# First projection fed from the unscaled, pre-transposed input in three pieces; value product of the attention moved behind the projection

## What is computed

```python
h = rmsnorm(x, norm1_g)
proj = h @ w_in + b_in                    # 1024 -> 4352 columns
qa, ka, va, qb, kb, vb, ga, gb = split(proj)
oa = neighborhood_attention(qa, ka, va, na_rpb)   # 8 heads of 64
ob = sliding_window_gqa(rope(qb), rope(kb), vb, swa_sinks)
merged = sigmoid(ga) * (oa @ w_up_a) + sigmoid(gb) * (ob @ w_up_b)
x = x + merged @ w_out
h2 = rmsnorm(x, norm2_g)
x = x + moe_clamped_swiglu(h2, ...)       # top 4 of 32 experts, 1024 -> 2048 -> 1024
return rmsnorm(x, final_g)
```

## Time and profile before

| | |
|---|---|
| runs | 1160.08, 1163.53, 1163.86 us |
| the profiled execution | 1160.33 us |
| its span on the core | 1158.4 us |
| TensorE busy in the span | 94% |
| VectorE, ScalarE, GpSimd busy | 22%, 12%, 1% |
| bytes moved | 436.4 MB |

### The profile page before, as it was taken

How to read it: one execution, slowest core, us unless ns; L and a number is a source line. 1 busy time by engine, 2 the same in 40 slices (tenths; PEclk the granted TensorE clock), 3 DMA queues, 4 the chain that set the end, 5 groups by cost and what they waited for, 6 DMA issues and landing times.

```text
span 1158.4 us, 13079 instructions
## 1 busy us (share of the span) xinstructions
PE 1087.3 (94%) x5169; PEld 475.6 (41%) x5169; DVE 250.2 (22%) x531; ACT 139.9 (12%) x267; POOL 16.3 (1%) x21
## 2 busy tenths in 40 slices
PE   7999999999999999999999999999999999999997
PEld 6887778633333333333333333233333333333332
DVE  2253532231111111111111111111111111211112
ACT  0121420210100000000000000000001111111111
POOL 0200000200000000000000000000000000000000
PEclk9999999999999999999999999999999999999999
DMA  8963373499999999999999999999999999999993
GB/s 280 354 257 109 100 291 145 186 398 390 430 427 429 429 427 429 429 427 429 429 427 429 429 427 429 429 427 429 429 427 429 428 426 427 430 428 428 427 430 136
DMA packets 42565, 436.41 MB, mean 377 GB/s; under 512 B 11650, under 2 KB 12084, under 8 KB 13396
## 3 DMA queue, kind: packets, MB, share of 16 engines
q1 hardware_dynamic: 42548, 436.16, 90.4%
HBM read 435.10 MB, written 1.05 MB: 377 GB/s over the span
## 4 chain that ended last, share of the span: by engine, by line
PE 60%; DMA 35%; DVE 2%; ACT 1%; issue 1%; POOL 0%; SPq 0%; DVEq 0%; POOLq 0%; ACTq 0%
DMA ring<-in_w 35%; PE bank L733 24%; PE bank L764 10%; PE bank L492 9%; PE bank L654 3%; PE bank L702 3%; PE bank L577 2%; PE bank L613 2%; PE bank L660 2%; PE bank L488 1%; DVE work L1090 1%; PE bank L539 1%; ACT held L1139 1%; PE bank L525 1%; PE bank L720 1%
## 5 line engine op out<-in xcount | busy, mean ns | idle before, releaser
L733 PE MATMUL bank<-ring,work 128*64 128x512 f32 x2048 | 452.5, 594 | 28.3 <-DMA ring<-in_w 27.6
L733 PEld LDWEIGHTS bank<-ring,work 128*64 128x64 f32 x2048 | 143.7, 137 | 316.4 <-issue 253.6
L764 PE MATMUL bank<-ring,work 128*64 128x512 f32 x1024 | 233.8, 598 | 18.1 <-DVE work L1090 18.1
L764 PEld LDWEIGHTS bank<-ring,work 128*64 128x64 f32 x1024 | 67.8, 136 | 140.7 <-issue 115.0
L1082 DVE TENSOR_SCALAR work<-bank 128x512 f32<-128x512 f32 x32 | 22.1, 691 | 435.0 <-PE bank L733 435.0
L492 PE MATMUL bank<-hT,ring 128*128 128x256 f32 x464 | 103.0, 381 | 0.8 <-DVE hT L833 0.8
L492 PEld LDWEIGHTS bank<-hT,ring 128*128 128x128 f32 x464 | 87.3, 190 | 16.1 <-issue 1.9
L1204 ACT ACTIVATE work<-work 128x512 f32<-128x512 f32 x32 | 20.1, 630 | 559.2 <-DVE work L1082 559.2
L1093 DVE COPY work<-bank 128x512 f32<-128x512 f32 x32 | 22.1, 692 | 253.7 <-PE bank L764 253.7
L654 PE MATMUL bank<-hT,work 128*64 128x512 f32 x264 | 64.6, 610 | 0.0
L702 PE MATMUL bank<-work 64*128 64x512 f32 x256 | 63.6, 615 | 0.9 <-DVE work L1093 0.9
(11 more groups left out here) (176 smaller groups left out, 451.2 us busy)
## 6 DMA issues: line engine op xcount, KB each, us to landing
ring<-in_w SPq DMA_DIRECT2D x182, 2048.0 KB, 21.6
ring<-in_w_in SPq DMA_DIRECT2D x17, 1024.0 KB, 12.9
held<-in_w SPq DMA_DIRECT2D x10, 1024.0 KB, 11.1
ring<-in_w SPq DMA_DIRECT2D x10, 1024.0 KB, 16.8
ring<-in_w_out SPq DMA_DIRECT2D x4, 1024.0 KB, 5.1
ring<-in_w_up_a SPq DMA_DIRECT2D x2, 1024.0 KB, 11.2
ring<-in_w_up_b SPq DMA_DIRECT2D x2, 1024.0 KB, 7.2
tables<-in_na_rpb SPq DMA_DIRECT2D x16, 96.0 KB, 4.9
```

The lines of the kernel that those rows point to most:

```text
L733: last = pe.matmul(bank[CAP * a:CAP * (a + 1), bk, :], kT, pairs[:, pair_of(k // 2), at + q * 512:at + (q + 1) * 512], start=False, stop=k ...
L764: last = pe.matmul(bank[CAP * a:CAP * (a + 1), BH, :], fT, pairs[:, pair_of(c), at + a * 512:at + (a + 1) * 512], start=f == 0, stop=f == ...
```

## The change

1. The host hands over `x` also transposed (`xT`, laid where `x` goes later), the columns `vec`, and the bias table at full size in plain order, with the mask in plain order too; so `from_right` and the transposes at the start go.
2. `xT` and chunk 0 of `w_in` are loaded in three alternating pieces: two blocks of 128 rows, two, and four (`FIRST`). VectorE multiplies a block by `norm1_g` into `xg1`, and `project_first` multiplies piece by piece. Chunks 0 and 1 use this unscaled input, chunk 2 and later use `hT`, which is `xg1` times the scale of each token.
3. The scale: ScalarE squares `xT`, VectorE sums over the blocks, TensorE sums over the partitions (`sum_squares`) inside chunk 1, GpSimd takes the power, VectorE makes two diagonal matrices, TensorE spreads them over the partitions (`spread_scale`), also inside chunk 1. VectorE multiplies what it reads of chunks 0 and 1 by it.
4. ScalarE's queue issues `vec`, `ident`, `v_bias` and `sink_b`. One DMA of 1.5 MiB takes the place of the sixteen of 96 KB. Row-ordered `x` (1 MiB) is loaded behind chunk 12, for the residual sum.
5. In the loop over c the order is `turn_probs`, `scores`, `project(c)`, `attend`. The first unit's scores stand at c = 5, the rotary step at c = 10, units 4 to 7 at c = 12 to 15, their transpositions at c = 13 to 16. VectorE reads an output one chunk later. PSUM banks are assigned anew (`BK`, `BF`, `BQ`, `BR`, `UPB`, `OUTB`).
6. The first lifting product no longer waits for the last gates and the last four outputs; the second and third take over these waits.

The diff, cut to its core:

```diff
+        xT = x.rearrange("p m d -> p (m d)").rearrange("p (k t) -> p k t", t=T)
+        xg1 = gates[:, 0:KD, :]
+        square = hT
...
-        ROPE_C = GATE_C
-        UNIT_C = [4, 6, 7, 8, 11, 12, 13, 14]
-        TURN_C = [6, 7, 8, 9, 12, 13, 14, 15]
+        ROPE_C = GATE_C + 1
+        UNIT_C = [5, 6, 7, 8, 12, 13, 14, 15]
+        TURN_C = [6, 7, 8, 9, 13, 14, 15, 16]
         unit_at = lambda table, c: table.index(c) if c in table else None
         LAST_PLAIN = TURN_C[-1]
-        BS, BT, BO, BK = 3, 5, 7, 2
+        BS, BT, BO, BK = 3, 5, 7, 3
+        BF, BQ, BR = 4, 6, 7
+        UPB = [4, 2, 0, 6]
+        OUTB = [2, 3, 0, 1]
+        FIRST = [slice(0, 2), slice(2, 4), slice(4, KD)]
...
+        def projected(c, a):
+            return half_(BF)[:, 1, :] if (c, a) == (0, 1) else half_(c % 3)[:, a, :]
...
-            for m in range(MT):
-                sp.dma_start(x[:, m, :], x_in[0, m * P:(m + 1) * P, :]).then_inc(x_landed[m], 16)
-            sp.dma_start(C("ident"), consts[:, CONST["ident"]]).then_inc(ident_landed, 16)
-            sp.dma_start(vec_rows[0:D_IN // P, :], b_in.rearrange("l (b p) -> (l b) p", p=P)).then_inc(vec_landed, 16)
-            for i, g in enumerate((norm1_g, norm2_g)):
-                at = D_IN // P + i * KD
-                sp.dma_start(vec_rows[at:at + KD, :], g.rearrange("l (b p) -> (l b) p", p=P)).then_inc(vec_landed, 16)
+            for n, ks in enumerate(FIRST):
+                cols = slice(ks.start * CW, ks.stop * CW)
+                sp.dma_start(xT[:, ks, :], xT_in[:, ks, :]).then_inc(xT_landed[n], 16)
+                sp.dma_start(ring[:, 0, cols], w_in[0][:, cols]).then_inc(first_landed[n] if n < 2 else landed[0], 16)
...
-            for n in range(PRE):
+            for n in range(1, PRE):
...
-                    sp.dma_start(v_bias[:, 0:NA_W], bcast(b_in, 2 * NA_W, NA_W)).then_inc(attn_small_landed, 16)
-                    sp.dma_start(v_bias[:, NA_W:], bcast(b_in, 4 * NA_W + P, P)).then_inc(attn_small_landed, 16)
-                    sp.dma_start(sink_b[:], bcast(swa_sinks, 0, HEADS)).then_inc(attn_small_landed, 16)
-                    for r in range(2):
-                        for hd in range(HEADS):
-                            at = hd * RPB + (NA_ROWS - 1 - 2 - r) * RPB_W + NA_COLS - 1
-                            src = bass.AP(na_rpb.tensor, at - (GRID_W - 1), [[1, GRID_W], [RPB_W, DR], [1, GRID_W]])
-                            dst = na_bias[r * GRID_W:(r + 1) * GRID_W, hd, :].rearrange("p (a c) -> p a c", c=GRID_W)
-                            sp.dma_start(dst, src).then_inc(bias_landed, 16)
+                    sp.dma_start(tables[:], na_rpb).then_inc(bias_landed, 16)
+                if n == SLOTS:
+                    sp.wait_ge(hT_scaled, KD)
+                    sp.dma_start(x, x_in[0].rearrange("(m p) d -> p m d", p=P)).then_inc(x_landed, 16)
...
-            power(0, slice(0, 1), 1)
-            power(0, slice(1, 2), 2)
-            pool.wait_ge(bias_landed, 16 * 2 * HEADS)
+            power(0, slice(0, MT), 1)
+            pool.wait_ge(bias_landed, 16)
...
-            pe.wait_ge(ident_landed, 16)
-            pe.wait_ge(vec_landed, 48)
-            pe.transpose(bank[:, 4, 0:n_vec], vec_rows[0:n_vec, :], C("ident")[0:n_vec, 0:n_vec]).then_inc(vec_done, 1)
-            for m in range(MT):
-                pe.wait_ge(h_ready, m + 1)
-                for a in range(2):
-                    for j in range(4):
-                        k = 4 * a + j
-                        last = pe.transpose(quarter(2 * m + a)[:, j, :], h[:, m, k * P:(k + 1) * P], C("ident"))
-                    last.then_inc(hT_done, 1)
-            pe.wait_ge(hT_ready, 2 * MT)
+            def project_first():
+                w = ring[:, 0, :].rearrange("p (k n) -> p k n", n=CW)
+                for n, ks in enumerate(FIRST):
+                    pe.wait_ge(first_landed[n] if n < 2 else landed[0], 16)
+                    for a in range(2):
+                        for k in range(ks.start, ks.stop):
+                            if a == 0:
+                                pe.wait_ge(xg1_ready, k + 1)
+                            last = pe.matmul(projected(0, a), w[:, k, a * P:(a + 1) * P], xg1[:, k, :],
+                                             start=k == 0, stop=k == KD - 1)
+                last.then_inc(chunk_used, 1)
+            def sum_squares():
+                pe.wait_ge(ones_set, 1)
+                pe.wait_ge(sq_sum_ready, 1)
+                for m in range(MT):
+                    last = pe.matmul(bank[:, BQ, m:m + 1], sq_sum[:, m * P:(m + 1) * P], ones[:, 0:1], start=True, stop=True)
+                last.then_inc(ssq_done, 1)
+            def spread_scale():
+                pe.wait_ge(diag_ready, 1)
+                for m in range(MT):
+                    last = pe.matmul(bank[:, BR, m * P:(m + 1) * P], ones[:], diag[:, m, :], start=True, stop=True)
+                last.then_inc(scale_done, 1)
...
-                if c % 3 == BK and c > ROPE_C:
-                    pe.wait_ge(rope_ready, 1)
                 w = ring[:, slot_of(c), :].rearrange("p (k n) -> p k n", n=CW)
                 pe.wait_ge(landed[slot_of(c)], landings(c))
                 dst = half_(c % 3)
+                src = xg1 if c == 1 else hT
                 for a in range(2):
                     for k in range(KD):
                         st = dict(start=k == 0, stop=k == KD - 1)
+                        if c == 2 and a == 0:
+                            pe.wait_ge(hT_scaled, k + 1)
+                        if c == 1 and (a, k) == (0, 4):
+                            sum_squares()
+                        if c == 1 and (a, k) == (1, 4):
+                            spread_scale()
...
                 if scored is not None:
                     scores(scored)
+                if c:
+                    project(c)
+                else:
+                    project_first()
...
                 if turned is not None:
                     attend(turned)
-                project(c)
...
-            pe.wait_ge(o_ready, UNITS)
-            pe.wait_ge(proj_read_act, N_IN - GATE_C)
             for n in range(N_UP):
                 c, branch = N_IN + n, n % 2
+                if n == 0:
+                    pe.wait_ge(o_ready, 4)
+                    pe.wait_ge(max_ready, UNITS)
+                if n == 1:
+                    pe.wait_ge(o_ready, UNITS)
+                    pe.wait_ge(proj_read_act, N_IN - 2 - GATE_C)
+                if n == 2:
+                    pe.wait_ge(proj_read_act, N_IN - GATE_C)
...
+                dve.wait_ge(vec_landed, 16)
+                for n, ks in enumerate(FIRST):
+                    dve.wait_ge(xT_landed[n], 16)
+                    for k in range(ks.start, ks.stop):
+                        g1 = vec[:, D_IN // P + k:D_IN // P + k + 1]
+                        dve.tensor_scalar(xg1[:, k, :], xT[:, k, :], g1, None, ALU.mult).then_inc(xg1_ready, 1)
+                dve.wait_ge(square_done, 3)
+                dve.tensor_reduce(sq_sum, square[:].rearrange("p k t -> p t k"), AX.X, ALU.add).then_inc(sq_sum_ready, 1)
+                dve.wait_ge(ssq_done, 1)
+                dve.tensor_scalar(msq[:, 0, :], bank[:, BQ, 0:MT], 1.0 / D, EPS, ALU.mult, ALU.add).then_inc(msq_ready, 1)
+                dve.wait_ge(ident_landed, 16)
+                dve.wait_ge(rstd_ready, 1)
                 for m in range(MT):
-                    if m == 1:
-                        dve.wait_ge(ssq_act, 1)
-                    dve.tensor_scalar(msq[:, 0, m:m + 1], ssq[:, 0, m:m + 1], 1.0 / D, EPS,
-                                      ALU.mult, ALU.add).then_inc(msq_ready, 1)
-                    dve.wait_ge(rstd_ready, m + 1)
-                    dve.tensor_scalar(h[:, m, :], x[:, m, :], rstd[:, 0, m:m + 1], None, ALU.mult).then_inc(h_ready, 1)
-            dve.wait_ge(ones_set, 1)
+                    last = dve.tensor_scalar(diag[:, m, :], C("ident"), rstd[:, 0, m:m + 1], None, ALU.mult)
+                last.then_inc(diag_ready, 1)
+                dve.wait_ge(scale_done, 1)
+                dve.wait_ge(xg1_ready, KD)
+                ch.link(dve.tensor_copy(kraw[:], half_(BR)[:, 0, :]))
+                scale = kraw[:].rearrange("p (o t) -> p o t", o=1).to_broadcast([P, 2, T])
+                for k in range(0, KD, 2):
+                    dve.tensor_tensor(hT[:, k:k + 2, :], xg1[:, k:k + 2, :], scale, ALU.mult).then_inc(hT_scaled, 2)
...
-                            last = dve.tensor_scalar(qaT[:, b, :].rearrange("p (r c) -> p r c", c=GRID_W),
-                                                     from_right(src[:, a, :]), bias, SCALE, ALU.add, ALU.mult)
+                            ch.link(dve.tensor_tensor(qaT[:, b, :], projected(c, a), kraw[:], ALU.mult))
+                            last = dve.tensor_scalar(qaT[:, b, :], qaT[:, b, :], bias, SCALE, ALU.add, ALU.mult)
...
+                if unit_at(TURN_C, c - 1) is not None:
```

(40 more changed lines are left out.)

63 lines of the change are left out of this document (22 added, 41 removed).

## The result

The changed kernel runs in 1153.48 us (median of five, 1152.46 to 1154.82); the kernel before, with five runs now, in 1162.16 (1160.01 to 1163.86). The ratio is 0.9929, interval 0.9914 to 0.9943: 0.7% faster, and the median is within 0.1 us of the forecast 1153.5. The profiled execution took 1152.46 us with a span of 1150.6, that is 7.8 less than the span before. Single executions of either kernel scatter by 2 to 4 us, so that an agreement to 0.1 us says little about the terms of the sum.

A forecast was written before the change was run, and what follows sets the result against it. TensorE's front part, up to the first lifting product, was taken to bound. Terms 3.6 + 0.95 + 2.45 + 1.0 = 8.0 us gave 1160.3 - 8.0 = 1152.3, raised for scatter to 1153.5 us; range 1149 to 1159.

The forecast's parts named there:

- What bounds the kernel: TensorE's progress up to the first lifting product at 163.68 us sets when loads become dense; the rest shifts rigidly.
- The start: Chunks 0 and 1: first product at 5.0 us, chunk 1 ends at 21.84 instead of 25.45; 3.6 us won, bounds 2.0 and 5.3.
- The loads don't bind: Chunk 0: last weight piece lands at 8.8 us, so loads alone would allow 12.3, before the forecast end of 13.98.
- The slow pace: TensorE in chunk 0: 4.0 us of slow work at the 1.2 GHz pace, costing 2.0 us.
- The Trainium skill's rule on transposes: Start: transposes don't raise the clock; the forecast said the trace disagrees, and by the page the result would be 2 us better.
- The attention: Attention units: 0.95 us from unit 0's scores at c = 5, 2.2 + 0.25 us from the moved value product.
- The hand-over: Before the lifting products: the 0.98 us wait for the last gates goes, 1.0 us won.
- The clock at the routing step: At 233 to 236 us: granted clock of 0.50 may last longer or vanish, 1.5 us either way.
- (a): Chunk 0: clock stays low as TensorE pauses between pieces; start loses 1.4 us, 1157.3 to 1160 us; chance 0.10.
- (b): Start held by `vec` or `xT` until 9 us; gain 4.0 us, 1156.3 to 1159.5; chance 0.05.
- (c): Whole kernel: gain hidden because the load stream alone sets the end, 1160 to 1163.5 us; chance 0.05.
- (d): Expert loads, 240 to 887 us: moved weights slow the dense stream, 6.5 us per 1%, 1172 at 3%; chance 0.04.

The follow-up runs named there:

- The delay: The changed kernel with eight unused products of 128x256 behind chunk 3: 1158.91 us, ratio 0.9961 to the kernel before.
- one piece: The changed kernel with xT and chunk 0 each loaded in one DMA (8 KB per partition) instead of three: 1160.64 us, one run.
- the experiment: The changed kernel with the value product back in front of the projection: 1155.86 us, ratio 0.9948 to the kernel before.
- second profile: The changed kernel unaltered, run once more for comparison on the same chip as others: 1154.28 us, ratio 0.9936 to the kernel before.
- three or two pieces: Two: the changed kernel with xT and chunk 0 in two 4 KB-row pieces, bias loads on SP, ten unused products ahead: 1153.04 us, ratio 0.9920.
- filler: Seven unused products at the wait for the chosen experts, added to the kernel before (1161.47 us) or the best version (1151.66); a second filler: four in the first expert (1161.81, 1152.10).

## Why the number was right, and where its steps were not

*What bounds the kernel.* Right: TensorE's front part moves the whole rest. The delay shows it at 3.5 us for 3.45, and the loads are still at 0 GB/s at 210 us.

*The start.* The term of 3.6 us was mis-sized: it measured 25.45 - 23.94 = 1.5 us in the profile of the change, below its own lower bound of 2.0 (with the scatter of the same start, up to 2.1). The step that failed is "The loads don't bind". The last piece, put at 8.8 us, landed at 12.36, and chunk 0 ended half a chunk behind it, as the forecast's own bound of 8.8 + 3.49 would have it: 12.41 + 3.72 = 16.13 instead of 13.98. The late landing came with short rows and with ScalarE's loads on a second queue; how much belongs to either isn't shown. That the landing in one piece, 8.67, is near the forecast's 8.8 doesn't prove the arithmetic either: the 8.8 counted all 0.41 MB of ScalarE's queue ahead of the last piece, and only 0.15 had moved.

The slow pace was forecast at 2.0 us. It cost 2.0 in the first sixteen instructions of the change and up to 3.1 where nothing interrupted it (10.07 against 6.98); I had bounded its length by the 4.5 us between the transposes and the first product of the kernel before. But where the last piece binds, this cost doesn't add to the end of chunk 0, since TensorE would otherwise have waited as much longer: with the slow pace gone and the landing as late, chunk 0 still ended at 15.64. In the profile of the change the forecast had counted a cost that was hidden and left out the wait that hid it.

The eight instructions inside chunk 1 took 0.78 us, and their inputs were hidden, as forecast; the sum over blocks took 3.67 us instead of 2.4 and stayed hidden.

*The Trainium skill's rule on transposes.* It speaks of the kernel before, and no new run bears on it; whether the transposes of the kernel before are of the kind that the page describes isn't shown either. What the new start shows agrees with the other half of the page of the Trainium skill ("TensorE: Matmul & The Clock Gate", Part 1), that an idle engine starts at the low clock and activity raises it: after ten unused products the first eight instructions of chunk 0 took 1.99 us, 0.25 each, where the first sixteen of the change took 5.51, 0.34 each.

*The attention.* Right: 0.95 + 2.45, of which the experiment confirms the 2.45 at 2.37; the 0.95 has no experiment of its own. No `turn_probs` waited for VectorE.

*The hand-over.* Right: the 0.98 us are gone. From the end of chunk 1 to the lifting products the change takes 133.69 us, the kernel before 138.23: 4.5 won, 4.4 forecast.

*The clock at the routing step.* It was named as 1.5 us either way and counted in the range only. It fell to the change's side: 1.66 us in the profile, where the kernel before had it and the change had not. This filled most of the 2.1 us that the start had lost, 1.5 + 4.5 + 1.7 = 7.8 with rounding. The agreement of 1153.5 with 1153.48 is in part luck: without the clock, the profiled difference is 6.1 instead of 8.0. The forecast of the median also had 1.2 us added to 1152.3 by judgement, for the scatter of the executions. In its second profile the change had the half clock too, for 1.65 us, and its span was 1152.5. The lowest execution of the change is 1152.4, of the kernel before 1159.8 in all comparisons. I read that as one such stretch in each execution of the kernel before and in some of the change's, which is argued from the spans and not shown, as only profiled executions show the clock's place. Of the eight profiled kernels with three or two pieces and no filler at the routing step, the change among them, four had it there and four had none.

*The medians* differ by 8.0 and 8.7 us, more than 6.1. What of the rest is the clock and what the rate of the load stream (its start after equal front parts varied by 0.4 to 0.9 us between profiles) stays open.

*Rivals.* (a) was the nearest to the truth in its place: TensorE did pause for a piece, but full pace came before chunk 0 was half done, and the start gained 1.5 instead of losing 1.4. (b), a start held to 9 us, did not happen: `vec` was used at 4.45. (c) is refuted by the delay. (d) had no part: 29.37 us per bound expert in both kernels.

**The best version** found is the change with the two bias loads on SP behind chunk 3 and ten unused products ahead of the first: ratio 0.9903 against 0.9936 for the change on the same chip. About 2 us of that difference are the earlier end of chunk 0; with a filler added the ratio was 0.9913 and 0.9912.

## What to carry to other kernels

Before a transfer is cut into pieces so that work may start earlier, price the pieces by loads of their own row length and with every queue that is busy at the same time: here 2 and 4 KB rows moved 313 GB/s where the forecast had 410. Two limits in a row don't add: where work ends a fixed time behind the last landing, a slow pace ahead of it costs nothing. So where two limits stand side by side, here landings and a slow clock, taking away one shows little; take both away in one experiment before dropping either. And when a forecast agrees with the clock on the wall, check its terms all the same: a start that was 2.1 us short and 1.7 us of clock that nobody had planned nearly cancelled here.

## Not expected of the hardware

Two queues that are both busy move nearly the same number of packets (313 and 323, 169 and 170 from 5 to 8 us), so the one with the longer rows moves most of the bytes: 0.73 MB beside 0.29 with rows of 2 and 4 KB on SP's queue, 1.17 beside 0.08 with rows of 8 KB.

In the kernel with one piece, GpSimd's masking of the table ran at the same time as the scaling of `hT` on VectorE, and the four multiplications of 128x512, 2.50 us in the change, took 5.05, so that TensorE waited for each pair:

```profile
24.57 6.61 POOL L441 TENSOR_TENSOR tables<-tables,held 128x384 f32<-128x384 f32 x5 [2.83 <-DMA tables<-in_na_rpb]
...
25.27 5.05 DVE L861 TENSOR_TENSOR hT<-held,kraw 128x512 f32<-128x512 f32 x4
27.57 0.73 PEld L509 LDWEIGHTS bank<-hT,ring 128*128 128x128 f32 x4 [0.61 <-DVE hT L861]
```

The change escapes this by little: its masking starts at 26.18 and its scaling ends at 25.27.

A sum over 2048 elements per partition that reads with a step of 256 elements and writes 256 results took 3.67 us, where one over 1024 neighbouring elements that writes four takes 1.22: 1.5 times as long per element. Whether the step or the number of results costs it isn't shown.

The granted clock is listed as 1.00 in the first 12 us of every profile, while single instructions of chunk 0, where no unused products came first, take 634 ns before and 379 ns after a point between 9 and 14 us. The later half clocks, at the routing step and in the second expert, are listed.
